# Splitting the fourth weight panel ahead of the norm, and running the first two output panels of the merge side by side

## The reference

```python
def rmsnorm(x, g):
    y = xf * lax.rsqrt(jnp.mean(xf * xf, axis=-1, keepdims=True) + RMS_EPS)
    return (y * g.astype(jnp.float32)).astype(x.dtype)

def swiglu(h, w13, w2):
    g, u = jnp.split(h @ w13, 2, axis=-1)
    return (jax.nn.silu(g) * u) @ w2

for i in range(DEPTH):
    h = rmsnorm(x, norm_mix_g[i])
    ...
    x = x + y
    x = x + swiglu(rmsnorm(x, norm_ffn_g[i]), f_w13[i], f_w2[i])
...
merged = jax.nn.sigmoid(a_gret) * y_ret + jax.nn.sigmoid(a_gmla) * y_mla
return merged @ w_o
```

## Time and profile before

| | us |
|---|---|
| median of 3 runs | 1759.53 (1757.08 to 1760.8) |
| the profiled execution's own time | 1752.1 |
| its span, first to last instruction | 1750.3 |
| PE busy | 1691.5 (97%) |
| PE weight loads busy | 1599.1 (91%) |
| DVE busy | 1227.7 (70%) |
| ACT busy | 971.9 (56%) |
| mean granted PE clock | 0.991 of full |

### The profile page before, as it was taken

How to read it: one execution, slowest core, us unless ns; L and a number is a source line. 1 busy time by engine, 2 the same in 40 slices (tenths; PEclk the granted TensorE clock), 3 DMA queues, 4 the chain that set the end, 5 groups by cost and what they waited for, 6 DMA issues and landing times.

```text
span 1750.3 us, 37337 instructions
## 1 busy us (share of the span) xinstructions
PE 1691.5 (97%) x13776; PEld 1599.1 (91%) x13776; DVE 1227.7 (70%) x2013; ACT 971.9 (56%) x1352; POOL 12.9 (1%) x20
## 2 busy tenths in 40 slices
PE   7999999999999999999999999999999999999997
PEld 7999999888999987569999999999999876799997
DVE  6887766586777587888776678776566665577764
ACT  4467745365775454206774446775454645468742
POOL 0000200000000000000000000000000000000000
PEclk9999999999999999999999999999999999999999
DMA  6567674433766554105666456667454432256662
GB/s 206 167 206 240 192 230 139 160 109 97 252 198 223 164 166 141 64 1 158 204 199 213 158 170 183 205 193 250 154 180 145 137 140 61 73 165 198 194 225 70
DMA packets 79545, 290.15 MB, mean 166 GB/s; under 512 B 9739, under 2 KB 12140, under 8 KB 79340
## 3 DMA queue, kind: packets, MB, share of 16 engines
q1 hardware_dynamic: 79468, 289.11, 52.2%
HBM read 288.03 MB, written 1.05 MB: 165 GB/s over the span
## 4 chain that ended last, share of the span: by engine, by line
PE 84%; DVE 11%; ACT 2%; issue 2%; DVEq 0%; DMA 0%; SPq 0%; ACTq 0%
PE bank L570 24%; PE bank L572 23%; PE bank L571 23%; DVE wlo L1516 3%; PE bank L858 2%; PE bank L845 1%; PE bank L799 1%; DVE conv_cv L1625 1%; DVE rinv L1522 1%; PE bank L954 1%; DVE hy_z L1765 1%; PE bank L1050 1%; ACT whi L1148 1%; PE bank L1060 1%; PE bank L1023 1%
## 5 line engine op out<-in xcount | busy, mean ns | idle before, releaser
L1148 ACT CAST whi<-raw 128x1024 fp32r<-128x1024 f32 (+1 forms) x490 | 539.3, 1102 | 328.4 <-PE bank L572 293.0
L570 PE MATMUL bank<-xq_h,whi 128*128 128x256 f32 x2384 | 666.9, 280 | 8.2 <-DVE wlo L1516 8.1
L571 PE MATMUL bank<-xq_h,wlo 128*128 128x256 f32 x2384 | 660.4, 277 | 0.0
L572 PE MATMUL bank<-xq_l,whi 128*128 128x256 f32 x2384 | 660.4, 277 | 0.0
L1516 DVE TENSOR_TENSOR wlo<-raw,whi 128x1024 fp32r<-128x1024 f32 (+1 forms) x491 | 629.9, 1283 | 5.4 <-ACT whi L1148 2.7
L570 PEld LDWEIGHTS bank<-xq_h,whi 128*128 128x128 f32 x2384 | 448.2, 188 | 19.3 <-DVE wlo L1516 12.7
L571 PEld LDWEIGHTS bank<-xq_h,wlo 128*128 128x128 f32 x2384 | 447.8, 188 | 1.5 <-issue 1.5
L572 PEld LDWEIGHTS bank<-xq_l,whi 128*128 128x128 f32 x2384 | 449.1, 188 | 0.0
L570 PE MATMUL bank<-ffn_hh,whi 128*128 128x256 f32 x880 | 242.9, 276 | 0.0
L571 PE MATMUL bank<-ffn_hh,wlo 128*128 128x256 f32 x880 | 242.9, 276 | 0.0
L572 PE MATMUL bank<-ffn_hl,whi 128*128 128x256 f32 x880 | 242.9, 276 | 0.0
(11 more groups left out here) (336 smaller groups left out, 2365.0 us busy)
## 6 DMA issues: line engine op xcount, KB each, us to landing
raw<-in_w SPq DMA_DIRECT2D x414, 512.0 KB, 3.6
raw<-in_w SPq DMA_DIRECT2D x80, 704.0 KB, 4.2
att_bias<-in_bias SPq DMA_DIRECT2D x4, 512.0 KB, 5.7
hy_w<-in_filt_w SPq DMA_DIRECT2D x8, 256.0 KB, 5.4
hy_decay<-in_decay SPq DMA_DIRECT2D x4, 512.0 KB, 4.4
mla_uq<-in_uq SPq DMA_DIRECT2D x1, 1152.0 KB, 5.4
x<-in_xT SPq DMA_DIRECT2D x1, 1024.0 KB, 5.9
out<-x SPq DMA_DIRECT2D x8, 128.0 KB, 2.0
```

The costliest lines, as they stand in the source:

```text
L570: pe.matmul(ps, whi[:, slot, wc], hi[:, k, cols], start=first, stop=False)
L571: pe.matmul(ps, wlo[:, slot, wc], hi[:, k, cols], start=False, stop=False)
L572: mm = pe.matmul(ps, whi[:, slot, wc], lo[:, k, cols], start=False, stop=last)
L1148: nc.scalar.copy(slices(whi, p % RING, k, to), raw_slices(p % RING, k, to)).then_inc(panel_hi, 1)
```

## The change

`norm_inv` gets the phase that follows and, in front of its wait for the root, makes the `wlo` of that phase's fourth panel (`split_fourth`). The phase's first step then leaves its split out: `steps` runs the first round of four steps by itself, with no split in step 0, and loops over the rest. This holds for the nine products named above. `in0` is as it was. Behind the merge, `w_o` runs its first two panels side by side (`merged`), and DVE makes the `wlo` of the third panel of `w_o` behind the last merged rows instead of ahead of them.

```diff
+        def merged():
+            ph = PH["w_o"]
+            for j in range(2):
+                pe.wait_ge(panel_lo, ph.p0 + j + 1)
+                pe.wait_ge(bank_free, ph.t0 + j + 1)
+            for k in range(K8):
+                pe.wait_ge(y_lo, YBASE["mrg"] + k + 1)
+                for j in range(2):
+                    slot = (ph.p0 + j) % RING
+                    ps = bank[(ph.b0 + j) % 4][:, Q]
+                    wc = slice(k * P, (k + 1) * P)
+                    pe.matmul(ps, whi[:, slot, wc], mg["yh2"][:, k, Q], start=k == 0, stop=False)
+                    pe.matmul(ps, wlo[:, slot, wc], mg["yh2"][:, k, Q], start=False, stop=False)
+                    mm = pe.matmul(ps, whi[:, slot, wc], mg["yl2"][:, k, Q], start=False, stop=k == K8 - 1)
...
+            for j in range(2, 8):
+                panel(ph, j // 4, j % 4, mg["yh2"], mg["yl2"], Q, None)
...
-        product("w_o", mg["yh2"], mg["yl2"], Q, (y_lo, YBASE["mrg"]))
+        merged()
...
-    def steps(eng, ph, first, n, step, chain=None, per=0, ahead=4, loop=True):
+    def steps(eng, ph, first, n, step, chain=None, per=0, ahead=4, loop=True, split_early=0):
...
-        if rounds > 1 and loop:
-            start = chain.n if chain else 0
-            with eng.Fori(0, rounds) as i:
+        if split_early:
+
+            for j in range(4):
+                one(0, j, None if j < split_early else ph.k)
+            alone = 1
+        if rounds - alone > 1 and loop:
+            start = chain.n - alone * per if chain else 0
+            with eng.Fori(alone, rounds) as i:
...
-        def norm_inv(norm, cols):
+        def split_fourth(ph):
+
+            split_lo(ph, 0, 0, 0, ph.k)
+
+        def norm_inv(norm, cols, ph=None):
+            if ph is not None:
+                split_fourth(ph)
             dve.wait_ge(root_ready, norm + 1)
...
-            dve_steps(ph, 0, ph.n, step)
+            dve_steps(ph, 0, ph.n, step, split_early=1)
...
-                split_lo(ph, 0, 0, m, K8)
+                if m:
+                    split_lo(ph, 0, 0, m, K8)
...
-            split_lo(ph_mo, 0, 0, j, K8)
+            if j < 3:
+                split_lo(ph_mo, 0, 0, j, K8)
...
+        split_lo(ph_mo, 0, 0, 3, K8)
         residual(PH["w_o"], ("ffn_w2", 0), A, norm, A)
-        norm_inv(norm, A)
+        norm_inv(norm, A, PH["up4"])
```

More of the change, by code:

```diff
@@ L896, in hyena @@
                 panel(PH["out2"], j // 4, j % 4, hy["yh"], hy["yl"], Q, None)
+        def merged():
[12 more added lines that the diff above has]
+                    mm = pe.matmul(ps, whi[:, slot, wc], mg["yl2"][:, k, Q], start=False, stop=k == K8 - 1)
+                    if k == K8 - 1:
+                        mm.then_inc(panel_used, 1)
+            for j in range(2, 8):
+                panel(ph, j // 4, j % 4, mg["yh2"], mg["yl2"], Q, None)
         def retention_in(norm):
@@ L1106, in _ @@
         assert norm + 1 == NORMS
-    def steps(eng, ph, first, n, step, chain=None, per=0, ahead=4, loop=True):
+    def steps(eng, ph, first, n, step, chain=None, per=0, ahead=4, loop=True, split_early=0):
         crossing = first + n == ph.n and ph.next_k != ph.k
         rounds = n // 4 - (1 if crossing else 0)
+        alone = 0
         def one(i, j, split):
             step(i, j, split)
-        if rounds > 1 and loop:
-            start = chain.n if chain else 0
-            with eng.Fori(0, rounds) as i:
+        if split_early:
[5 more added lines that the diff above has]
+            with eng.Fori(alone, rounds) as i:
                 if chain:
@@ L1125, in steps @@
         else:
-            for i in range(rounds):
+            for i in range(alone, rounds):
                 for j in range(4):
@@ L1498, in _, with dve_steps @@
         mask_bias()
-    def dve_steps(*args):
-        steps(nc.vector, *args, ahead=3)
+    def dve_steps(*args, **early):
+        steps(nc.vector, *args, ahead=3, **early)
     @block.vector
@@ L1607, in short_conv @@
             link(V.memset(cm["cu"][:], 0.0))
-            dve_steps(ph, 0, 8, scaled(ph, 0, 8, lambda j, m: cm["c"][:, m, :]))
+            dve_steps(ph, 0, 8, scaled(ph, 0, 8, lambda j, m: cm["c"][:, m, :]),
+                      split_early=1 if layer else 0)
             if layer == 0:
@@ L1818, in multiply @@
                     dve.wait_ge(hs["Y"], 2 * n + f + 1)
-            dve_steps(ph, 0, 4, conv_step, link, 8)
+            dve_steps(ph, 0, 4, conv_step, link, 8, split_early=1)
             for p in range(4, 24):
@@ L1870, in decay_product @@
                 V.tensor_tensor(decay_of(h), decay_of(h), rx["e2"][:, h % 2, :], ALU.mult).then_inc(re["E"], 1)
-            dve_steps(ph, 0, 4, scaled(ph, 0, 4, lambda j, m: rt["t"][:, m, A]))
+            dve_steps(ph, 0, 4, scaled(ph, 0, 4, lambda j, m: rt["t"][:, m, A]), split_early=1)
             dve.wait_ge(re["lg"], 1)
@@ L2045, in _ @@
                 wing_weights(0)
-            norm_inv(norm, A)
+            norm_inv(norm, A, PH[f"in{layer}"] if layer else None)
             norm += 1
@@ L2056, in _ @@
             residual(PH[f"out{layer}"], ("ffn_g", layer * C), A, norm, A)
-            norm_inv(norm, A)
+            norm_inv(norm, A, PH[f"up{layer}"])
             norm += 1
@@ L2062, in _ @@
                      B if last else A)
-        norm_inv(norm, B)
+        norm_inv(norm, B, PH["in_ret"])
         norm += 1
```

## The result

| | median us | lowest to highest | runs |
|---|---|---|---|
| kernel before | 1758.16 | 1748.14 to 1764.42 | 12 |
| changed kernel | 1766.09 | 1760.1 to 1776.4 | 12 |

A forecast was written before the change was run, and what follows sets the result against it. TensorE, carrying 84% of the chain of waits, was taken to bound the kernel. Norms 7.6 us plus merge 3.1 gave 10.7 us off the median of 1759.5: 1748.8 us forecast, range 1745.0 to 1755.5.

The forecast's parts named there:

- the pace of loads is the unit for what follows: Weight loads take 0.1135 us each, from 96 loads of mla_out; used to price the time lost in stops.
- The splits ahead of the norm: At nine norms, moving the fourth panel's `wlo` split into DVE's idle time removes TensorE's stop: 7.6 us together.
- in2: At this norm taps limit the gain to 0.35 us; a stop of some 0.6 us remains before the fifth panel.
- `mean_sq`: In the norm, its start stays put against the root; more than 0.3 us later would show the prediction wrong.
- The merge: At w_o, the third panel starts at 1536.65 instead of 1539.79: 3.1 us gained, 1.7 if the clock falls.
- The clock rival: The clock falls in the new 1.87 us stop before w_o: gain 9.3, time 1750.2 us; chance 0.12.
- The rival that the stop moves on: Behind the norms, stops move to later panels and norms keep only a quarter: gain 5.1, 1754.4 us; chance 0.12.
- The code fetch rival: Longer TensorE code makes loops of up4 and down4 refetch, at most 2.0 us a turn: 1776.8 us; chance 0.03.
- The range: Whole kernel: 1745.0 to 1755.5 us, taking in the clock, half the moved-stop rival and the runs' 3.7 us spread.

The follow-up runs named there:

- merge only: Changed kernel with the nine early splits ahead of the norms undone, side by side w_o panels kept: 0.9975 of the kernel before, median 1758.58 us.
- before with wait at the sum: Kernel before, plus TensorE waiting for the end of each norm's sum of squares; stops at the fourth panels remain: ratio 1.0007, median 1757.81 us.
- changed three times: The changed kernel itself, measured three times against the kernel before: ratios 1.0054, 1.0015 and 1.0054; medians 1766.09, 1761.24 and 1770.2 us.
- splits only: Changed kernel with the merge undone, w_o panels one after the other, nine early splits kept: 0.9989 of the kernel before, median 1758.08 us.
- wait at the sum, no stop behind it: Changed kernel, plus TensorE waiting for the end of each norm's sum of squares; measured twice: 0.9916 and 0.9928 of the kernel before.
- wait behind the second panel: Changed kernel, plus TensorE waiting for its last matmul of the first two panels before the third: 0.9985 of the kernel before, median 1760.46 us.
- rounded sum: Changed kernel with the norm's sum of squares in the panels' rounded type, one matmul in place of two: 0.9969 of the kernel before, median 1750.65 us.
- a second sum last: Kernel before, plus one more plain float32 product behind the fourth panel in the five up products, not awaited: ratio 1.0161, median 1786.48 us.
- a second sum last, awaited: Kernel before with the extra float32 product behind the fourth panel of five up products, TensorE waiting for its end: ratio 1.0048, median 1767.85 us.
- the third measurement: The changed kernel run a third time, beside the kernel before on the same chip: ratio 1.0054, median 1770.2 us.

## Why the prediction was wrong

**The step that failed** is the first of the working: "the pace of loads is the unit for what follows", 0.1135 us each, from the 96 loads of mla_out. It was taken as a constant of the kernel, and every removed stop was then worth its length. But the pace is one of two, and the stop for `wlo` had a second effect that no term held: it stood right behind the sum of squares and in the up products mostly turned the slow pace that this left into the quick one. The kernel measured 1.0054 of the time before, with four of five blocks at 0.1178 us a load. Counted over the profiled executions:

| what stands between the sum and the block | quick blocks |
|---|---|
| stop at the fourth panel (before, merge only, before with wait at the sum) | 12 of 15 |
| nothing (changed three times, splits only) | 7 of 20 |
| wait at the sum, no stop behind it | 10 of 10 |
| wait behind the second panel, no stop at the fourth | 2 of 5 |
| rounded sum, nothing behind it | 4 of 5 |
| a second sum last | 0 of 5 |
| a second sum last, awaited | 5 of 5 |

The two runs with a second sum add to the first row: between the stop and that sum their fourth panel was quick in ten of ten, which makes it 22 of 25. The effect is one of the place: at in2 and in3 the same kind of stop left the quick pace in only 3 of 10 cases, and in the kernel before in neither.

From 12 of 15 to 7 of 20 is 0.45 of five blocks of 7 us, some 16 us more, against the 9 or so that the stops gave back: 7 us net, beside 7.9, 3.6 and 11.8 measured. This is an estimate from few draws, and it does not hold of each kernel: splits only has the stops removed as well, and measured no loss (0.9989).

**Point by point.**
- *The splits ahead of the norm* were sized about right. The stops as a whole fell by 7.5, 7.7 and 7.0 us in the three profiles, beside 10.7 forecast. 1.4 of these 10.7 were matmuls at the lower clock, which count as busy; that leaves 9.3 beside 7.0 to 7.7. Part of the rest lies in the counting. At up0 the stop is 1.14 us by the loads, as the prediction has it, but the matmul behind it (timeline of TensorE, before) shows only 0.86 of idle, since the records of matmuls outlast their distance and the first one behind the stop is longer:

```profile
120.05 0.38 PE L570 MATMUL bank<-xq_h,whi 128*128 128x256 f32 x1 [0.86 <-DVE wlo L1516]
```

- *The size at equal pace.* The profiled executions in which all five blocks are quick can be set side by side, though each is a single one and the stretches outside the blocks had their own draws: before 1752.1 us, the changed kernel with the wait at the sum 1740.97 and 1744.39. That is 11.1 and 7.7 us less, with nine waits in it, beside the 10.7 forecast. What the prediction priced was there; what it did not know of took it away.
- *in2* did as said: 0.56 us of idle at the fifth panel. *`mean_sq`* at up0 stayed within 0.05 us of its distance to the sum.
- *The merge* was right. In the third measurement's profile mla_out begins at 1524.59 and the third panel of w_o at 1542.93: 18.34 us, where before took 1539.79 - 1518.43 = 21.36. That is 3.0 of the 3.1 forecast. In the first profile of the changed kernel it took 20.09, since TensorE's clock was down at the start of mla_out (granted 0.62 from 1538 to 1542), a place that the change doesn't touch, and since w_o ran at the slow pace: its 48 loads took 5.64 us, 0.1175 each, at a granted clock of 1.00.
- *The clock rival* did not come true: w_o behind its stop of 1.96 us ran at full clock. *The rival that the stop moves on* held at in2 alone, as priced.
- *The code fetch rival* gave the sign but not the cause. The Trainium skill's rule on taken branches ("Runtime: NRT & Kernel Launch", Instruction fetch mechanics) would have shown as stops in the loops of up4 and down4; the stretch from 1600 to 1720 has no idle time in the three profiles of the changed kernel, and its count is one of the same two as everywhere else.
- *The range* rested on a spread of 3.7 us in three runs. Twelve runs of the kernel before spread over 16, which would be two or three blocks more or less at the slow pace.

**What could have been seen.** The trace of before, which was at hand, holds both paces. The same matmul of 128x256 took 276 ns for `ffn_hh` and 281 for `hy_yh`, and the loads on the two sides of the stop of the earlier trace rows stand 0.118 and 0.113 apart. The spread of 16 us, which only the later runs showed, belongs to it: a kernel whose runs spread so far with the same instructions has a cause for that, and a change of 10 us has to be weighed against it.

## What to carry to other kernels

Where TensorE bounds a kernel, read its pace (loads in a stretch without a stop) on both sides of each stop before you price the stop: removing it may also remove what restored the pace. If a float32 product stands in a dense stream of rounded ones, try a wait for its end, or round it where the loss in exactness can be borne; here the wait showed 4.2 us of idle weight loads and brought the changed kernel from 1.0054 to 0.9928 of the time before. And take profiles of two executions of the kernel before that lie far apart in time: what differs between two executions of the same code is not in the code's own chain of waits.

## What the runs showed of the hardware

- Matmuls of 128x256 with a weight load each ran at 113.3 or at 117.8 ns a pair, both at granted clock 1.00 (2.4 GHz), and kept to one of them for up to 1584 pairs. Two executions of one kernel differ by which blocks have which.
- A plain float32 product of 256 columns in such a stream, not awaited, left the slow pace in five of five cases as the second sum, and as the norm's sum in 29 of 41 cases behind a quick stretch. One in the rounded type kept a quick stretch quick in five of five, and two of three stretches at the slow pace turned quick.
- A wait for the float32 product's end left the quick pace in 29 of 29 cases: 24 sums of 256 columns in three profiles (the two of the changed kernel with the wait, and before with it) and five second sums. The spread of those runs leaves room for others in executions without a profile.
- The Trainium skill ("TensorE: Matmul & The Clock Gate", Back-to-back issue gap) gives N / 2.4 + 2.5 ns for an isolated matmul at full clock, which for 256 columns makes an estimate of 109.2. Both paces here, with a weight load for each matmul, lie above that estimate, by 4 and by 9 ns.

What in TensorE holds the pace, and why the product leaves the slow one, stays open: no run here changed the distance between the weight loads and the matmuls by itself. Nor is it known why a stop elsewhere in the stream gives now the one and now the other pace.
